# Reordered attention steps, moved gate rows and moved small projections in a four-layer float32 kernel

## The reference, cut to what matters

```python
# layers 0 and 1: modulated norm, one projection, a mixer, a gated output projection
x = x + gate[:, None] * jnp.matmul(y, w_out[layer])
if need_ctx:                       # layer 0
    x_ctx = x_ctx + c_gate * jnp.matmul(y_ctx, w_out[layer])
# layer 0's mixer: global attention (softmax over all 768 keys) beside a long-convolution branch ("hyena")
# layer 1's mixer: windowed attention with a sink beside neighbourhood attention with a bias
# softmax attention, per head:
p = jax.nn.softmax(jnp.einsum('bqhd,bkhd->bhqk', q, k) * dh ** -0.5 + bias, axis=-1)
o = jnp.einsum('bhqk,bkhd->bqhd', p, v)
# layers 2 and 3: three branches (a sparse attention with compressed keys "NSA", a latent attention "MLA",
# a forgetting attention "FOX"), merged by gates; then a memory attention; then an MLP with a squared relu
```

## Time and profile before

| | us |
|---|---|
| median of 3 runs | 3131.53 |
| lowest, highest | 3130.09, 3137.03 |
| the profiled execution: its time | 3130.09 |
| the profiled execution: its span, first to last instruction | 3128.2 |
| PE busy | 2902.4 |
| DVE busy | 1669.2 |
| ACT busy | 1071.9 |
| POOL busy | 448.4 |

### The profile page before, as it was taken

One profiled execution on the slowest core, in us unless ns is written; L12 is line 12 of the kernel. 1 busy time (PEld: TensorE's weight loads), 2 busy tenths in 40 slices (PEclk: granted clock), 3 DMA queues, 4 the chain that ended last, 5 costly groups with the idle time before them and its releaser, 6 DMA issues.

```text
span 3128.2 us, 43506 instructions
## 1 busy us (share of the span) xinstructions
PE 2902.4 (93%) x17412; PEld 2328.7 (74%) x17412; DVE 1669.2 (53%) x3179; ACT 1071.9 (34%) x1872; POOL 448.4 (14%) x401
## 2 busy tenths in 40 slices
PE   5889999899997898998999899999899999899998
PEld 2477774688984486485888689898566688779988
DVE  6855657764577744845335642426655423653344
ACT  3433335123136521634222431322454323332231
POOL 3200003231004520402020000000222111000000
PEclk8999999999999999999999999999899999999999
DMA  5433220223223043022324232324111323132331
GB/s 171 148 126 95 95 88 1 81 82 106 67 86 60 26 118 89 1 63 67 98 84 135 68 98 92 94 95 96 38 42 34 93 96 102 54 108 95 91 98 68
DMA packets 245423, 262.00 MB, mean 84 GB/s; under 512 B 12818, under 2 KB 227970, under 8 KB 245096
## 3 DMA queue, kind: packets, MB, share of 16 engines
q1 hardware_dynamic: 227808, 203.93, 21.7%
q0 software_dynamic: 12544, 45.08, 4.1%
q10 hardware_dynamic: 4872, 10.21, 1.5%
HBM read 245.04 MB, written 13.11 MB: 83 GB/s over the span
## 4 chain that ended last, share of the span: by engine, by line
PE 53%; DVE 8%; issue 2%; ACT 1%; DMA 1%; POOL 0%; SPq 0%; DVEq 0%; ACTq 0%; POOLq 0%
PE PS L346 29%; PE PS L3707 10%; PE PS L156 3%; PE PS L3606 2%; PE PS L1179 2%; PE PS L1168 2%; PE PS L1155 2%; DVE S L1206 1%; DVE HL L294 1%; DVE S L2593 1%; DVE S L2589 1%; DVE S L1234 1%; ACT HL L287 1%; PE PS L3368 1%; DMA S<-in_w_in 1%
## 5 line engine op out<-in xcount | busy, mean ns | idle before, releaser
L346 PE MATMUL PS<-xT,HL 128*128 128x512 f32 (+1 forms) x3552 | 792.2, 384 | 14.2 <-DVE HL L294 6.0
L294 DVE TENSOR_TENSOR HL<-S,HL 128x2048 fp32r<-128x2048 f32 (+2 forms) x204 | 423.5, 2081 | 671.1 <-ACT HL L287 671.1
L346 PEld LDWEIGHTS PS<-xT,HL 128*128 128x128 f32 x3552 | 644.7, 188 | 154.6 <-DVE HL L294 7.5
L287 ACT ACTIVATE HL<-S 128x2048 fp32r<-128x2048 f32 (+2 forms) x204 | 351.5, 1729 | 705.9 <-PE PS L346 287.1
L3707 PE MATMUL PS<-HL,hd 128*128 128x256 f32 x3072 | 370.3, 283 | 0.1
L3707 PEld LDWEIGHTS PS<-HL,hd 128*128 128x128 f32 x3072 | 369.4, 191 | 0.9 <-PE PS L3707 0.5
L1265 ACT ACTIVATE S<-S,S 128x256 f32<-128x256 f32 (+5 forms) x292 | 189.2, 648 | 188.4 <-DVE S L1206 181.2
L1300 POOL TENSOR_SCALAR S<-S,S 128x512 f32<-128x512 f32 (+4 forms) x104 | 179.9, 1730 | 392.0 <-DVE S L1221 228.5
L1168 PEld LDWEIGHTS PS<-S,S 128*128 128x128 f32 (+1 forms) x1048 | 113.5, 141 | 144.4 <-issue 44.9
L1168 PE MATMUL PS<-S,S 128*128 128x128 f32 (+1 forms) x1048 | 169.7, 289 | 43.9 <-DVE S L1234 12.7
L346 PE MATMUL PS<-h_high,HL 128*128 128x512 f32 (+1 forms) x768 | 201.3, 348 | 0.1
(11 more groups left out here) (406 smaller groups left out, 3938.9 us busy)
## 6 DMA issues: line engine op xcount, KB each, us to landing
S<-in_mlp_w_up SPq DMA_DIRECT2D x32, 1024.0 KB, 5.6
S<-in_mlp_w_down SPq DMA_DIRECT2D x32, 1024.0 KB, 5.2
S<-in_w_in SPq DMA_DIRECT2D x28, 1024.0 KB, 5.2
S<-in_w_ada SPq DMA_DIRECT2D x24, 1024.0 KB, 5.1
S<-in_w_gate SPq DMA_DIRECT2D x24, 1024.0 KB, 5.2
S<-in_w_in SPq DMA_DIRECT2D x36, 512.0 KB, 5.2
S<-in_w_mix_out SPq DMA_DIRECT2D x8, 1024.0 KB, 5.7
spectra<-S POOLq DMA_DIRECT2D x24, 256.0 KB, 4.8
```

Source lines behind the costliest of these rows:

```text
L287: m = a.activation(high, raw, ACT.Copy)
L294: m = v.tensor_tensor(low, raw, high.bitcast(F32), ALU.subtract)
L346: m = pe.matmul(dst, l[x], r[y], start=(i == 0 and j == 0), stop=(i == n - 1 and j == 2))
```

## The change

Six edits in one diff:

1. `gates(0, ...)` moves from ahead of the barrier to behind `hyena_gate`; it writes two plain tiles instead of parts of UC, and its 4 copies go to DVE and ACT in turn instead of all to ACT.
2. `gates` calls `dve_turn()` for each half row. For layer 1 that is two calls instead of one, so every later use of the counter gets the other engine.
3. The due time of a norm becomes `end + i + late`. For the causal jobs this is the same; for the others the norm of tile i comes at i + 0.6 instead of at the smaller of i + 1.6 and nq - 0.4, so tile i's norm stands directly behind its own scores (and a turn that is due by then) instead of behind the next tile's.
4. In the chunk list of layers 2 and 3 the small `narrow` chunk comes ahead of `kp`'s.
5. The NSA projections become narrow, compressed(0), kp, compressed(1), narrow_turn, branch_gates, vv.
6. `forget_logs` moves ahead of the transposes of the latent.

```diff
-                 [(768, 896), (1024, 1152)], [(1280, 1304), (1816, 1848), (2616, 2620)], [(896, 1024), (1152, 1280)]]
+                 [(1280, 1304), (1816, 1848), (2616, 2620)], [(768, 896), (1024, 1152)], [(896, 1024), (1152, 1280)]]
...
-    def gates(l, dst, on_v=None):
+    def gates(l, dst):
...
-            b, on_v = bank(), dve_turn() if on_v is None else on_v
+            b, on_v = bank(), dve_turn()
...
-                steps += [(end + i, 0, n, "scores", q), (end + min(i + 1.6, nq - 1 + late), 1, n, "norm", q)]
+                steps += [(end + i, 0, n, "scores", q), (end + i + late, 1, n, "norm", q)]
...
-    GB = [[UC[:, t, 512:1024] for t in ts] for ts in ((0, 1), (2, 5))]
-    gates(0, GB, False)
     f = barrier()
     tx = load_x(f)
...
     hyena_gate()
+    GB = [sb(BIG + 12800, 1024), sb(BIG + 13824, 1024)]
+    gates(0, GB)
     v.wait_ge(*tx)
...
-    gates(1, [[GB[0][:, 0:512], GB[0][:, 512:1024]]])
+    gates(1, GB)
...
+        t_narrow = project3_T([(0, 60, [(narrow[0:60, :], 0, 60)])])
+        compressed(0, gx0, t_gx0)
         project3_T([(i * 128, 128, [(kp[:, i, :], 0, 128)]) for i in range(2)])
-        compressed(0, gx0, t_gx0)
-        t_narrow = project3_T([(0, 60, [(narrow[0:60, :], 0, 60)])])
         compressed(1, gx1, t_gx1)
-        project3(xT, range(4), 256, lambda t: [(vv[:, t, :, :].rearrange("p b c -> p (b c)"), 0, 256)])
         narrow_turn()
         branch_gates()
+        project3(xT, range(4), 256, lambda t: [(vv[:, t, :, :].rearrange("p b c -> p (b c)"), 0, 256)])
...
         project3_T([(j * 128, 128, [(fq[:, j, :], 0, 128)]) for j in range(2)], scale=-0.125)
+        t_ll = forget_logs()
         pe.wait_ge(*t_cq)
         transposed([([cq[:, t, k * 128:k * 128 + 128] for t in range(4)], [(cT_[:, k, :], 0, 128)]) for k in range(4)])
         t_cT = evac_token()
-        t_ll = forget_logs()
```

More of the change, by code:

```diff
@@ L567, in dve @@
                     v.wait_ge(*full)
-                    v.tensor_copy(dst[c][h], PS[:, b, :]).then_inc(*vl.event())
+                    v.tensor_copy(dst[c][:, h * 512:h * 512 + 512], PS[:, b, :]).then_inc(*vl.event())
         def act():
@@ L573, in act @@
                     a.wait_ge(*full)
-                    a.activation(dst[c][h], PS[:, b, :], ACT.Copy).then_inc(*al.event())
+                    a.activation(dst[c][:, h * 512:h * 512 + 512], PS[:, b, :], ACT.Copy).then_inc(*al.event())
         tensor()
@@ L963, in dve @@
                         v.wait_ge(*added_by[at - 2])
-                    v.tensor_tensor(tmp[at % 2], PS[:, b, 0:256], GB[0 if t < 4 else 1][n // 2][:, n % 2 * 256:n % 2 * 256 + 256], ALU.mult
+                    v.tensor_tensor(tmp[at % 2], PS[:, b, 0:256], GB[0 if t < 4 else 1][:, n * 256:n * 256 + 256], ALU.mult
                                     ).then_inc(*vl.event())
@@ L2459, in program @@
     g.tensor_copy(gates1, GB[0]).then_inc(*gl.event())
-    out_proj(yT, parts, 4, [[gates1[:, 0:512], gates1[:, 512:1024]]], t_y, grid(AREA + 12288, 2, 256), turned=True,
+    out_proj(yT, parts, 4, [gates1], t_y, grid(AREA + 12288, 2, 256), turned=True,
              moved=[moved, ld_scr.all()])
```

## The result

The changed kernel takes 3164.53 us (median of 4 runs, 3159.11 to 3173.37), the kernel before beside it 3133.7 (4 runs, 3130.09 to 3137.03). The ratio is 1.0101, with a 95% interval from 1.0074 to 1.013: slower by 1.0%, some 32 us (the medians are 30.8 apart), where the prediction had 3161 and a range from 3142 to 3174. The profiled execution, which is not among the four, took 3164.42 us.

What follows compares the result with a forecast made beforehand. PE was taken to bound the kernel, with 53% of the chain that ended last. Terms 12.3 + 2.6 - 0.8 + 5.1 + 5.0 + 7.8 = 32.0 on 3130.09 gave 3162, kept at 3161, range 3142 to 3174.

Steps and rivals of the forecast that it cites:

- First jobs: First attention jobs of layers 0 and 1: DVE stands still for the exponentials' sums, +3.85 and +4.6 us.
- Later jobs: Later attention jobs: norm and wait exceed DVE's slack, +1.5 us in layer 0, +2.7 windowed, +2.2 neighbourhood.
- What is won back: Attentions: the last tile's norm no longer queues behind another, shortening PE's waits for ACT's scaling, -2.5 us.
- Gates: Layer 0: gate products leave the last inverse transform's cover and delay `out_proj`, +2.6 us, plus 1 for the clock.
- NSA projections: Layers 2 and 3: PE waits for `kp`'s load and split, branch gates' chain hides under `vv`, +5.1 us for both.
- `forget_logs`, +5.0: Layers 2 and 3: copies PE waits for stand behind its table load and logarithm, +2.5 us each, +5.0 for both.
- Clock, +7.8: Behind PE's new idle times: half clock costs 1.7 us per `kp` and `project_from`, 1 at the gates, +7.8.
- rival (a): The clock doesn't fall in the new gaps: 3154 us; chance 0.26.
- (b): Only the attention term is real, projections and `forget_logs` hide as ACT's and DVE's queues run ahead: 3142 us; chance 0.12.
- (c): An earlier norm relieves PE, all its 17.6 us of waits on norms go away: 3124 us; chance 0.04.
- (e): Nothing shows, all lies in layers' slack: 3131 us; chance 0.04.
- (d): DVE never catches up in later attention jobs, 16 us; clock low twice as long, 17: 3175 us; chance 0.14.

Runs made afterwards that it cites:

- experiment 1: The kernel before with only the norms' due time changed: 3144.32 us against 3131.93, ratio 1.0039.
- experiment 9: The kernel before with the norms' new due time for every job but an attention's first: 3136.54 us against 3131.79, ratio 1.0019.
- experiment 2: The kernel before with only layer 0's gates moved behind `hyena_gate`, in two plain tiles, all four copies on ACT: 3134.04 us, ratio 0.9999.
- the second execution: The changed kernel once more, unchanged, against the kernel before: 3160.82 us against 3129.86, ratio 1.0091.
- experiment 3: The kernel before with only the chunk order and the order of the NSA projections changed, `vv` moved too: 3138.67 us, ratio 1.0017.
- 10: The kernel before with `forget_logs` moved, plus 34 unread products in PE's idle time in front of `project_from`: 3140.52 us against 3131.79, ratio 1.0021.
- 11: The kernel before with the NSA edits, plus 36 unread products in PE's idle time in front of `kp`: 3142.23 us against 3131.79, ratio 1.0031.
- 4: The kernel before with only `forget_logs` moved ahead of the transposes of the latent: 3142.39 us, ratio 1.0032.
- 7: The kernel before with copy turns flipped, early norm for 2-tile jobs, `vv` behind the branch gates, `forget_logs` behind the first `project_from`: 3127.52 us, ratio 0.999.
- 12: The kernel before with the early norm for 2-tile jobs and `vv` behind the branch gates: 3125.88 us against 3131.79, ratio 0.9988.

## Why the prediction was right

The forecast held in its sum and in most of its terms; one step of the norm term was wrong, and two errors of the sum cancel. Term by term, with what was predicted first:

- **First jobs, +3.85 and +4.6.** Measured +3.93 and +4.55 in the changed kernel, by the mechanism named (the wait of 1.14 to 1.37 for the sums). Right. The low clock inside them cost nothing of its own: scores of 1.56 us took up to 2.93 us there, the low stretches were not equally long in the three executions with this edit, and the job took the same to 0.03 us, as DVE paces it.
- **Later jobs, +1.5, +2.7 and +2.2.** Measured in experiment 1: +0.8, +3.9 and +2.4. The neighbourhood jobs are right. In layer 0 the job behind the first gives back 0.2 instead of losing 0.5; 0.3 of that hangs on the first job's new order, as without it (experiment 9) the job is 0.05 longer than before, and why its own norms cost so little is not shown. The windowed jobs were undersized (1.3 each, not 0.9). The step that failed here is that the copy of a turn covers the wait in slots 2 to 4: in slots 3 and 4 DVE still waits 0.54 us each in layer 0 and 1.03 and 0.82 in the windowed jobs. The prediction had these waits only in its upper bound; in layer 0 and in the neighbourhood jobs DVE's slack takes in most of them.
- **What is won back, -2.5.** PE's wait on ACT's scaling fell by 2.4, and layer 0's small jobs by 1.3. The other recoveries are in stages where runs without the edit differ by about 1 us too, so their size stays open.
- **Sum of the norm edit, +12.3.** The runs say +12.2 (7 to 17), which holds some clock and is too wide to test the single terms.
- **Gates, +2.6 and 1 of clock.** Measured +3.8 in the stage, 1.33 of it clock. In experiment 2 and in the second execution the same products lost 1.9 to 2.0 to the clock. Right, though only the traces show it.
- **Engine turn, -0.8.** -1.05 in its place. Right in place and size.
- **NSA projections, +5.1 for both layers.** `kp` started 11.15 and 10.46 us behind `hidden(1)`, where 11.2 and 10.6 were predicted; the branch gates' chain went under `vv` as said. Without the slower `kp` the way from `hidden(1)` to the compressed scores grew by 3.15 and 2.19 us in the changed kernel, 5.3 together. Right, though the runs of experiment 3 say +5.3 (2 to 8.5) with the clock in it, and +8.5 had been foretold for that.
- **`forget_logs`, +5.0.** PE's waits grew from 2.04 to 4.58 and from 1.80 to 4.60, 5.3 together, and the edit alone gave 5.4. Right. The logarithm starts again 0.01 us behind the table load's end (1394.11 + 1.28 to 1395.40), so no drain shows here either.
- **Clock, +7.8.** Behind the new idle times the products took 2.27 and 1.37 us more (`kp`), 1.69 and 2.60 more (`project_from`) and 1.33 more (the transposes of the hyena branch): 9.3. Right in kind and nearly in size: rival (a) fell. The upper bound of 17 is not quite what it is said to be, as twice the term is 15.6. The Trainium skill, page "TensorE: Matmul & The Clock Gate", section "HAM oscillation — how this bites in real kernels", says that PE falls to half its clock when it stands idle; experiments 10 and 11 agree, 14.02 against 11.28 us for the same products. Not every idle time does it here, as the 2.82 us at 339 and the 2 us in front of `project_from` show.

Rivals (b), (c) and (e) fell with experiments 1, 3 and 4. Of (d), the attention's 16 us lie inside the interval of the runs of experiment 1; against it speak the job lengths, 14.4 us in all before what is won back behind them, and the clock's 9.3 where (d) had 17.

The terms as measured add up to 12.2 + 2.5 - 1.05 + 5.3 + 5.3 + 9.3 = 33.6, and a little of the clock stands in it twice; the span grew by 34.4 in one execution and by 30.3 in the other. Two things in the profile were not in the prediction. They have opposite signs and nearly cancel, which was luck. The 4.2 us ahead of layer 0's attention came mostly by chance (0.7 in the other execution). And layer 3's NSA and MLA parts grew by only 2.8 us where the terms give 2.3 + 2.5 and the clock's 3.4: the projections alone grew by 3.6, but the clock ran low in the parts behind them in the profiled execution of the kernel before, in places where it didn't after. I had taken the clock's cost from the new idle times alone, as if the rest of its low stretches stayed in place. Between two executions of one kernel they moved the span by 4 us.

## What to carry to other kernels

When two engines work at a tile in turns, ask where the consumer's next instruction stands in its queue relative to the moment at which its input is ready: one slot too early stalls the queue for the whole latency, and in the first job, where nothing else is queued, at full price. An idle time of PE costs more than its length, as the products behind it run slower; here 4.2 to 4.9 us of idle time cost 1.4 to 2.8 us on top each time, and some 2 us of it cost 1.7 now and then. An edit that bundles a gain with a loss (branch gates under `vv`, and `narrow` ahead of `kp`) should be taken apart: here the first half alone was faster by 0.17%, and the whole slower. In 7 and 12, which hold this half too, the gain is 0.1% and the interval reaches zero, so it is small and not sure.

## What the runs showed of the hardware

- The same product sequence, at the same place in the program, ran at a granted clock of 0.57 in one execution and 1.00 in another (339 to 351 us); the two were 3.6 us apart at the attention behind it. An idle time of PE of 2.82 us stood ahead of it in all 14 profiled executions, and the clock fell in 3. A change of less than some 4 us in all is told from such traces by stages only, not by their spans.
- A float32 product of 128 x 128 is two instructions of 0.115 us each in the trace (8.30 us for 36 products, shown as x72).
- Behind an idle time of 4.2 to 4.9 us `kp` ran 1.4 to 2.8 us longer in all six cases. Behind one of 4.6 us `project_from` ran 1.5 to 2.6 us longer in all six, so the length of the idle time alone doesn't set the loss. Behind 1.8 to 2.05 us it ran 1.7 us longer in 3 of 20.
- In `forget_logs` the table load of ScalarE took 1.28 us; it started 0.01 us behind the exponential's end (1393.88 + 0.22 to 1394.11), and the logarithm 0.01 us behind the load's.
